# A third projection chunk accumulated in two transpose banks while the adaptive norm's weights stream in, and an even spacing of the projection units between the norm's units

## The reference, cut to what matters

```python
mod = silu(c) @ w_ada + b_ada                    # w_ada: 2048 x 6144
shift, scale, gate = split(mod, 3)
h = rmsnorm(x, ln_gain) * (1 + scale) + shift    # adaptive norm, 384 x 2048
proj = h @ w_in                                  # 2048 x 8336: q_a, ckv, krope, g_a, q_b, k_b, v_b, ...
...                                              # latent attention (A) and sparse attention (B)
y = concat(rmsnorm(o_a) * silu(g_a), rmsnorm(o_b) * silu(g_b))
out = x + gate * (y @ w_out)                     # then a last rmsnorm
```

## Time and profile before

| | before |
|---|---|
| median of the runs | 1035.64 us (1033.83 to 1037.22) |
| the profiled execution | 1035.65 us, its span 1033.6 us |
| PE busy | 955.5 us, 92% of the span |
| DVE, ACT, POOL busy | 419.0, 338.4, 91.3 us |
| moved by DMA | 183.28 MB, mean 177 GB/s |
| mean granted TensorE clock | 0.976 |

### The profile page before, as it was taken

How to read it: one execution, slowest core, us unless ns; L and a number is a source line. 1 busy time by engine, 2 the same in 40 slices (tenths; PEclk the granted TensorE clock), 3 DMA queues, 4 the chain that set the end, 5 groups by cost and what they waited for, 6 DMA issues and landing times.

```text
span 1033.6 us, 14404 instructions
## 1 busy us (share of the span) xinstructions
PE 955.5 (92%) x5851; PEld 822.5 (80%) x5851; DVE 419.0 (41%) x857; ACT 338.4 (33%) x621; POOL 91.3 (9%) x165
## 2 busy tenths in 40 slices
PE   3798689999999999998999999999999899699995
PEld 0466377899998788888998998899888889588884
DVE  2222243336332244432324722368334344845452
ACT  2322342333312242323314422333222234633332
POOL 1000004102100000111111100000001000400000
...
GB/s 324 385 290 339 345 171 200 148 150 150 154 112 92 81 91 125 153 204 135 105 102 220 208 206 165 105 127 184 226 155 223 161 83 278 244 212 133 122 62 122
DMA packets 128402, 183.28 MB, mean 177 GB/s; under 512 B 29408, under 2 KB 79256, under 8 KB 127184
## 3 DMA queue, kind: packets, MB, share of 16 engines
...
...
## 4 chain that ended last, share of the span: by engine, by line
PE 82%; DMA 6%; ACT 3%; DVE 3%; issue 2%; SPq 1%; POOL 1%; ACTq 0%; POOLq 0%; DVEq 0%
PE proj L1624 31%; PE proj L1613 30%; DMA raw<-in_w_in 2%; DMA raw<-in_w_ada 2%; PE bankS L1613 2%; SPq L642 1%; PE bankO L1702 1%; PE bankO L1711 1%; PE bankO L1604 1%; PE bankO L1927 1%; PE proj L1604 1%; PE bankS L1828 1%; DVE w_lo L1192 1%; ACT w_hi L864 1%; PE bankT L1843 1%
## 5 line engine op out<-in xcount | busy, mean ns | idle before, releaser
L1192 DVE TENSOR_TENSOR w_lo<-raw,w_hi 128x1024 fp32r<-128x1024 f32 (+2 forms) x168 | 198.5, 1186 | 240.0 <-ACT w_hi L864 239.5
L864 ACT ACTIVATE w_hi<-raw 128x1024 fp32r<-128x1024 f32 (+2 forms) x168 | 171.8, 1028 | 215.3 <-PE proj L1613 102.3
L1624 PE MATMUL proj<-hT_hi,w_hi 128*128 128x384 f32 x640 | 222.8, 348 | 1.1 <-ACT misc L864 1.1
L1624 PE MATMUL proj<-hT_hi,w_lo 128*128 128x384 f32 x640 | 215.3, 336 | 0.0
L1624 PE MATMUL proj<-hT_lo,w_hi 128*128 128x384 f32 x640 | 215.1, 336 | 0.0
L1613 PE MATMUL proj<-w_hi,hT_hi 128*128 128x512 f32 (+2 forms) x496 | 193.7, 391 | 21.4 <-DVE w_lo L1192 12.3
L1613 PE MATMUL proj<-w_hi,hT_lo 128*128 128x512 f32 (+2 forms) x496 | 188.9, 381 | 0.0
L1613 PE MATMUL proj<-w_lo,hT_hi 128*128 128x512 f32 (+2 forms) x496 | 188.8, 381 | 0.0
L1613 PEld LDWEIGHTS proj<-w_hi,hT_hi 128*128 128x128 f32 x496 | 95.2, 192 | 42.1 <-DVE w_lo L1192 16.0
L1624 PEld LDWEIGHTS proj<-hT_hi,w_hi 128*128 128x128 f32 x640 | 121.2, 189 | 9.1 <-issue 7.0
L1624 PEld LDWEIGHTS proj<-hT_lo,w_hi 128*128 128x128 f32 x640 | 121.1, 189 | 0.7 <-issue 0.2
...
## 6 DMA issues: line engine op xcount, KB each, us to landing
...
raw<-in_w_ada SPq DMA_DIRECT2D x128, 256.0 KB, 6.5
...
```

The source lines that it names most:

```text
L864: return nc.scalar.activation(out, in_, func, scale=scale, **kw)
L1192: V.tensor_tensor(w_lo[:, u % RAW, 0:w], raw[:, u % RAW, 0:w], w_hi[:, n % SPLIT, 0:w].bitcast(F32), ALU.subtract).then_inc(lo_ready, 1)
L1624: ins = mm(banks[blk][:, 0:TOK], w[:, n, cols], a[:, kt, :], start=first and n == m == 0, stop=final and n == per - 1 and m == 2)
```

## The change

- `ga` 1 (4 units) leaves the dense list and is put among the `ada` units: its first unit right after `ada` 1's last, its second after `ada` 2's last, its third after `ada` 3's last, its fourth just ahead of `ckv`. It accumulates in banks S and T, which the transposes used until then.
- Each of the quarters 1, 2 and 3 now reads: 5 `ada`, `kb`, 4 `ada`, `ga` 0, 4 `ada`, `kb`, 3 `ada`, `ga` 1. After `ada` 3 stand `ga` 1.2, `kb` 0.6, `kb` 0.7, `ga` 0.3, `ga` 1.3.
- To clear the banks, all twelve `xT` move ahead (six into quarter 0, six into the first six units after it), `modT` moves to bank O, the accumulator itself, at the quarter's last unit, and the first unit of the next quarter waits until DVE has read it. The `uvT` steps and their loads stand seven unit numbers later, three more than the four inserted units account for, with `uvT` 0 behind the eviction of `ga` 1.
- The dense list is four units shorter: 28 `gate` units stand inside it and four after it, where it was 29 and three.

```diff
--- before.py
+++ after.py
@@ -63,10 +63,10 @@
 def chunks():
 
     out = [("ada", q, 1, 1) for q in range(4)]
-    out += [("kb", 0, 2, NT), ("ga", 0, 4, 2), ("ckv", 0, 2, NT), ("m0", 0, 2, NT), ("m1", 0, 2, NT)]
+    out += [("kb", 0, 2, NT), ("ga", 0, 4, 2), ("ga", 1, 4, 2), ("ckv", 0, 2, NT), ("m0", 0, 2, NT), ("m1", 0, 2, NT)]
     out += [("qn", j, 4, 2) for j in range(4)]
     out += [("kb", 1, 2, NT)] + [("vb", j, 2, NT) for j in range(2)]
-    out += [("ga", j, 4, 2) for j in range(1, 4)]
+    out += [("ga", j, 4, 2) for j in range(2, 4)]
     for kind in ("qi", "qb", "gb"):
         out += [(kind, j, 4, 2) for j in range(4)]
     out += [("gate", r, 1, 1) for r in range(2)]
@@ -87,20 +87,17 @@
         c = CHUNK_OF[kind, j]
         return [(c, k) for k in range(KT // CHUNKS[c][2])]
 
-    keys, gates = of("kb", 0), of("ga", 0)
+    keys, first, second = of("kb", 0), of("ga", 0), of("ga", 1)
     out = of("ada", 0)
     for q in range(1, 4):
         ada = of("ada", q)
-        out += ada[:6] + [keys[2 * q - 2]]
-        if q < 3:
-            out += ada[6:10] + [gates[q - 1]] + ada[10:13] + [keys[2 * q - 1]] + ada[13:]
-        else:
-            out += ada[6:]
-    out += [keys[5], gates[2], keys[6], keys[7], gates[3]]
-    ga1, gate0 = CHUNK_OF["ga", 1], CHUNK_OF["gate", 0]
-    for c in range(CHUNK_OF["ckv", 0], ga1):
+        out += ada[:5] + [keys[2 * q - 2]] + ada[5:9] + [first[q - 1]] + ada[9:13] + [keys[2 * q - 1]] + ada[13:]
+        out.append(second[q - 1])
+    out += [keys[6], keys[7], first[3], second[3]]
+    ga2, gate0 = CHUNK_OF["ga", 2], CHUNK_OF["gate", 0]
+    for c in range(CHUNK_OF["ckv", 0], ga2):
         out += of(*CHUNKS[c][:2])
-    dense = [u for c in range(ga1, gate0) for u in of(*CHUNKS[c][:2])]
+    dense = [u for c in range(ga2, gate0) for u in of(*CHUNKS[c][:2])]
     gate = of("gate", 0) + of("gate", 1)
     for n, u in enumerate(dense):
         out.append(u)
@@ -131,6 +128,8 @@
             mine = [4]
         elif (kind, j) == ("ga", 0):
             mine = [3, 4]
+        elif (kind, j) == ("ga", 1):
+            mine = [NPB + 1, NPB + 2]
         elif kind == "wo":
 
             mine = [(ring + n) % NPB for n in range(NPB)] + [NPB + 1]
@@ -152,7 +151,7 @@
 
 
 STEP_BANKS = {
-    "gains": "S", "bias": "O", "xT": "T", "uvT": "S", "modT": "S", "ckT": "T", "kiT": "S", "qrT": "T", "qrsT": "TO",
+    "gains": "S", "bias": "O", "xT": "T", "uvT": "S", "modT": "O", "ckT": "T", "kiT": "S", "qrT": "T", "qrsT": "TO",
     "ukT": "T", "kn": "O", "vm": "O", "mp": "S", "mt": "T", "mv": "O", "ql": "O", "krc": "T",
     "st": "T", "ss": "S", "sp": "S", "so": "O", "oa": "O", "ysq": "O",
     "kic": "T", "ip": "S", "is": "T", "iacc": "O", "kl": "TO", "dp": "S", "dt": "T", "dv": "O",
@@ -179,28 +178,27 @@
 
     put(0, ("ld_x", 0))
     put(1, ("ld_small", 0))
-    run(5, "xsq", NT)
-    put(8, ("xr", 0))
-    run(9, "xT", NT)
+    run(3, "xsq", NT)
+    put(5, ("xr", 0))
+    run(6, "xT", 6)
     put(12, ("gains", 0))
-    for g in range(1, 4):
-        for t in range(NT):
-            put(LAST_UNIT["ada", g - 1] + (3, 5, 11)[t], ("xT", NT * g + t))
+    u = LAST_UNIT["ada", 0]
+    for n in range(6, 12):
+        put(u + n - 5, ("xT", n))
 
     for q in range(4):
-        u = LAST_UNIT["ada", q] + 1
+        u = LAST_UNIT["ada", q]
         put(u, ("modT", q))
         for n in range(MQ):
-            v = u + (1, 1, 2, 2)[n] if q < 3 else u + n // 2
-            put(v, ("h", MQ * q + n))
-            put(v + 1, ("hl", MQ * q + n))
+            put(u + 1 + n // 2, ("h", MQ * q + n))
+            put(u + 2 + n // 2, ("hl", MQ * q + n))
     u = LAST_UNIT["ada", 3]
     put(u + 4, ("ld_const", 0))
     put(u + 4, ("bias", 0))
     put(u + 8, ("bias_rd", 0))
     for n in range(HEADS):
-        put(u + 2 + 2 * n, ("ld_uv", n))
-        put(u + 5 + 2 * n, ("uvT", n))
+        put(u + 5 + 2 * n, ("ld_uv", n))
+        put(u + 8 + 2 * n, ("uvT", n))
 
     u = LAST_UNIT["ckv", 0] + 1
     put(u, ("ckn", 0))
@@ -517,7 +515,7 @@
 
     ps = [nc.alloc_psum_tensor(f"proj{n}", [P, 512], F32) for n in range(NPB)]
     bank = {n: nc.alloc_psum_tensor(f"bank{n}", [P, 512], F32) for n in "STO"}
-    ps += [bank["O"], bank["S"]]
+    ps += [bank["O"], bank["S"], bank["T"]]
 
 
     bias_d = nc.dram_tensor("bias_scratch", [HEADS, NDELTA], F32).ap()
@@ -534,7 +532,7 @@
 
     raw_loaded = [sem(f"raw_loaded{n}") for n in range(RAW)]
     hi_ready, lo_ready, unit_used = sem("hi_ready"), sem("lo_ready"), sem("unit_used")
-    proj_free = [sem(f"proj_free{n}") for n in range(NPB + 2)]
+    proj_free = [sem(f"proj_free{n}") for n in range(NPB + 3)]
     full = {b: sem(f"bank_{b}_full") for b in "STO"}
     free = {b: sem(f"bank_{b}_free") for b in "STO"}
 
@@ -1221,9 +1219,9 @@
             emptied(dve, "gains", 0)
             b_cols = gcol[:, 32:64].rearrange("p (a k) -> p a k", a=2)[:, :, MQ * n:MQ * (n + 1)]
             for a in range(2):
-                ins = V.tensor_tensor(part[:, a], bank["S"][:, P * a:P * (a + 1)].rearrange("p (k j) -> p k j", j=32)[:, :, 0:9],
+                ins = V.tensor_tensor(part[:, a], bank["O"][:, P * a:P * (a + 1)].rearrange("p (k j) -> p k j", j=32)[:, :, 0:9],
                                       b_cols[:, a].unsqueeze(2).broadcast_to([P, MQ, 9]), ALU.add)
-            ins.then_inc(free["S"], 1)
+            ins.then_inc(free["O"], 1)
             emptied(dve, "modT", n)
             V.scalar_tensor_tensor(out=part[:, 1], in0=part[:, 1], scalar=1.0, in1=gcol[:, MQ * n:MQ * (n + 1)]
                                    .unsqueeze(2).broadcast_to([P, MQ, 9]), op0=ALU.add,
@@ -1589,7 +1587,12 @@
                 if first and BEFORE[c][n]:
                     pe.wait_ge(proj_free[BANKS[c][n]], BEFORE[c][n])
 
-            if (kind, j) in (("kb", 0), ("ga", 0)) or kind == "wo":
+            if kind == "ada" and first and j:
+                emptied(pe, "modT", j - 1)
+            if (kind, j) == ("ga", 1) and first:
+                emptied(pe, "gains", 0)
+                emptied(pe, "xT", 11)
+            if (kind, j) in (("kb", 0), ("ga", 0), ("ga", 1)) or kind == "wo":
 
                 pe.wait_ge(sem("hT_ready"), per * (k + 1) + (KT if kind == "wo" else 0))
             if kind in WHOLE:
@@ -1645,6 +1648,8 @@
 
         def uvT(h_):
             pe.wait_ge(sem(f"wuv_in{h_ % 2}"), 16 * (h_ // 2 + 1))
+            if h_ == 0:
+                moved(pe, "ga", 1)
             out = take("uvT", h_, "S")
             for q in range(CB):
                 ins = tr(out[:, P * q:P * (q + 1)], wuv[:, h_ % 2, P * q:P * (q + 1)], eye[:])
@@ -1652,13 +1657,15 @@
 
         def modT_(n):
             moved(pe, "ada", n)
-            out = take("modT", n, "S")
+            out = take("modT", n, "O")
             for a in range(2):
                 ins = tr(out[:, P * a:P * (a + 1)], modA[:, n % 2, P * a:P * (a + 1)], eye[:])
-            ins.then_inc(full["S"], 1)
+            ins.then_inc(full["O"], 1)
 
         def ckT(t):
             pe.wait_ge(sem("ckvn_ready"), NT)
+            if t == 0:
+                moved(pe, "ga", 1)
             out = take("ckT", t, "T")
             for q in range(CB):
                 ins = tr(out[:, P * q:P * (q + 1)], ckvn[:, t, P * q:P * (q + 1)], eye[:])
```

## The result

The changed kernel takes 1043.03 us (median of 20 runs, 1036.6 to 1054.0), the kernel before 1034.40 us on the same chip (20 runs). The ratio is 1.007, with a 95% interval of 1.0054 to 1.0087: the change makes the kernel slower by 0.7%, some 7 us. The ratio leaves out the execution of 1054.0 us, which counts as a slow one, and is therefore a little smaller than the 8.6 us between the medians. The forecast was 1028.5 us with a range of 1021.5 to 1035.0. The profiled execution of the changed kernel is a quick one among its runs, 1040.02 us with a span of 1037.9 us, against 1035.65 and 1033.6 before; the traces therefore account for 4.3 us of span.

What follows compares the result with a forecast made beforehand. It took the kernel as bound by PE except in the first 170 us. 1035.65 - 14.2 (dense list and start) + 0 (`uvT`) + 7.0 (tail) = 1028.45, given as 1028.5 us, range 1021.5 to 1035.0.

Steps and rivals of the forecast that it cites:

- Dense list, -16.7 us: Dense list: four units of 4.17 us leave a stretch where PE is full, so 16.7 us go.
- `modT` 1 at 73.1 us: Start, quarters 0 and 1: `modT` 1 comes 0.8 us later than its 72.3 us, bounds 0 and +2.8.
- Quarters 2 and 3 at 29.8 us each: Start: each quarter of 20 units takes 29.8 us, between a floor of 27.1 and a ceiling of 30.7.
- The same chain of `h` steps hides behind the same one `ga` unit: Behind `modT` 3: 21.4 us as before plus 4.2 for `ga` 1.3, 25.6 us to `ckv`.
- `uvT`, 0: Around `ckv`'s start: the later first `w_uv` load costs 0, within -1.2 and +3 us.
- The tail, +7.0 us: End of dense list: more `y` steps and splits precede `gate` 1's eviction, costing 7.0 us, bounds 4.5 and 9.
- parts 1 and 2: Dense list and start together: 16.7 us gained less 2.5 lost, 14.2 us, bounds 10.4 to 20.4.
- wrong if `ckv` starts after 163 us: Start: sign that the forecast fails; `ckv`'s first matmul was expected at 157 to 160 us.
- slower: Rival at the start: lower ring rate, at 290 GB/s a quarter lasts 36.2 us, time 1041.2 us; chance 0.06.
- The start eats most of it: Rival: quarters at their ceiling and quarter 1 late, 1033.8 us, no change; chance 0.15.
- the lower bound: Start's best case: `ckv` at 152.1 us, a gain of 20.4 us for parts 1 and 2.

Runs made afterwards that it cites:

- gate_first: Changed kernel with DVE's addition of gate 1 moved to the row of `gate` 1.12, ahead of `y` 8; 1034.91 us, ratio 1.0024.
- gates_spread: Changed kernel with `gate` units also behind the first and third dense unit; 1035.37 us, ratio 1.0010.
- hl_first: Changed kernel with the last quarter's `h` and `hl` steps in one row, ahead of both splits; 1031.05 us, ratio 0.9974.
- before_gate: Kernel before with the gate sum placed ahead of the reciprocal, nothing else; 1028.12 us, ratio 0.9931.
- even_only: Changed kernel with `ga` 1 back in the dense list, even spacing kept, last quarter's `h` and `hl` steps in one row; 1038.25 us, ratio 1.0045.
- third_out: even_only with the older unit places, the gate sum ahead and the accumulator's copy ahead of the next split; 1022.83 us, ratio 0.9905.
- old_places: all_three with the start's units at the kernel before's places inside each quarter; 1023.40 us, ratio 0.9902.
- all_three: Changed kernel with last quarter's `h` and `hl` steps, gate 1's addition and ACT's accumulator copy all moved ahead; 1026.52 us, ratio 0.9927.

## Why the prediction was wrong

It gave 1028.5 us and faster at 0.77. The sign was wrong. By its own steps, against the traces:

1. *Dense list, -16.7 us.* Right: from `ckv` to kload -17.1. The cover at `gate` 0's eviction held; PE has no wait there.
2. *`modT` 1 at 73.1 us.* Right within 0.9 (73.96).
3. *Quarters 2 and 3 at 29.8 us each.* Met by the second (29.6, at 361 GB/s for a forecast of 352), 5.0 short for the third (34.8). Two things were not in the working: PE waited 3.1 us for the weights of `ga` 0.2 and its matmuls behind that ran slow, and ACT's copy of the accumulator stood behind splits for late loads, 3.5 us. The size also varies: gate_first, whose start is the same code, had 32.8 and 32.7 us, gates_spread 32.0 and 34.6, hl_first, the same up to `modT` 3, 30.3 and 33.5. So that the second met the forecast is luck of this trace. In these four the sum of the two was 63.8 to 66.6 us, not 59.6, so this term was some 4 to 7 us too low in each. The point that the forecast started from scatters as much: `modT` 3 of the old start came at 134.4 and, in before_gate, at 139.15 us.
4. *"The same chain of `h` steps hides behind the same one `ga` unit", 25.6 us from `modT` 3 to `ckv`.* This is the step that failed by its mechanism. It took 34.35 us, and 31.2 and 34.3 in the other two traces of that start. The chain of arithmetic is the same, but between its links stand splits that wait for a buffer, and the even spacing had moved `kb` 0.5 from behind the last `ada` unit into the quarter. With that unit went the slack of those buffers. hl_first takes the splits out of the chain and has 23.7 us from `modT` 3 to `ckv` (137.50 to 161.24), less than forecast. That the splits cost the time is shown by this; that the absent `kb` 0.5 took the slack is read from the rows of the two kernels, as no run puts it back alone.
5. *`uvT`, 0.* Right: PE's wait for w_uv was 0.5 us.
6. *The tail, +7.0 us.* Right in mechanism and nearly in size: +8.2 from ysum on, less the 1.1 us of `gate` units that only changed sides, makes 7.1. The two waits stand as forecast, 6.5 and 4.8 us for 8 and 6, and the gate sum came after 19.1 us, forecast 18 to 19. What the text didn't say is that the cost was in the order alone (gates_spread), and that the kernel before pays 7.9 us of the same kind (before_gate).

The sum of the misses: 14.1 us at the start (16.6 for 2.5), -0.4 in the dense list, -2.3 behind it (the tail's 7.1 less what the stretch ahead of ysum gained, which isn't the change's), makes 11.4, the distance from -7.2 to +4.3. The gain of parts 1 and 2 was bounded at 10.4 to 20.4 us; it was 0.5 in this pair of traces, and with `ckv` of before_gate as the old start it would be 5.2. By the prediction's own mark, "wrong if `ckv` starts after 163 us", the failure is at the start, and the rival called *slower* had the right deciding point (`ckv` after 168.6 us) with the wrong cause: it wanted 290 to 300 GB/s in the quarters, which had 361 and 326. *The start eats most of it* had the right cause in part, with too small a price.

On the Trainium skill's figure, DMA: Bandwidth & Descriptors, section Bandwidth (about 358 GB/s a core on the HBM side): quarter 2 of the changed kernel ran at 361 GB/s over 29.6 us and quarter 0 before at 387 GB/s over 15 us, so the trace still doesn't agree with it as a ceiling. The same section gives this figure as the share of a core when both cores of an HBM domain stream, and this program runs on one core, so as a rule against the lower bound it didn't bear on the case. The third quarter, which came out long, was not bound by it either: it ran at 326 GB/s.

What stays open: why the even places cost, and whether they do at all by more than even_only's 0.45%. `modT` 3 came 8.0 us earlier in third_out than in even_only, and 4.0 earlier in old_places than in all_three, one trace each; but third_out has two more edits, the same start scatters by 4.8 us in the kernel before and before_gate, and the timed difference of all_three and old_places isn't beyond the measurement. That the first `kb` unit of a quarter stands before its load has landed is argued from the w_lo waits, not shown.
